# Pairs of key heads and partition groups of samples in a hybrid decoder layer

## Chip, cores and metric

The kernel runs on one core of a Trainium2 chip. The metric is device microseconds of one execution. TensorE is called PE in the rows, its weight loads PEld, VectorE DVE, ScalarE ACT, GpSimd POOL, and the queue that issues most transfers SP.

## What is computed

One layer of a decoder: 512 prompt tokens and 8 samples of one token each (with 2048 past positions) go through the same weights. Four mixers (two gated linear attentions A and B, pooling C, sparse attention D) are gated, projected and added, then an MLP follows. The change touches the sample's step of A and B, and D:

```python
# A, B, per sample: S = S * exp(log_f) + k v^T ; o = S^T q
o = jnp.einsum('bthk,bhkv->bthv', qd, S)
# D: 8 query heads in 2 groups (key heads) of 4, head dimension 64; three branches, each a softmax over its keys
sc = jnp.einsum('bqhgd,bchd->bqhgc', qb, kc)      # compressed keys, one per 16 tokens
ss = jnp.einsum('bqhgd,bhqkpd->bqhgkp', qb, ks)   # selected blocks of 64 tokens, top 16 (prompt: all are selected)
sw = jnp.einsum('bqhgd,bkhd->bqhgk', qb, wb[:, :, 0])   # window of 512
o  = gb[..., 0:1] * o_cmp + gb[..., 1:2] * o_slc + gb[..., 2:3] * o_win
```

All data are fp32. For the 512 prompt tokens the selected and the window branch are both causal attention with keys and values of their own.

## The kernel before

Each engine has its own program, and they meet at semaphores. TensorE's program alternates between two kinds of work. The first is the **special work** of the mixers, written out in order. The second is **dense work**: projections with 128x1024 weight tiles, each product made of three matmuls in a reduced fp32 format (high x high, low x high, high x low; a "triple", L618 to L624; L651 for outputs by token). `tick(name, i)` stands in every engine's program at the same places: on TensorE it makes triples until a table (`CUM`, from the quotas of `SECTIONS`, L169) is met, on SP it loads weight tiles whose slot came free (`LD_AT`), one tick later ScalarE casts them to the high part (`upper`, L1179, the cast is L1183), one more tick later GpSimd makes the low part (`lower`, L2126). VectorE or ScalarE evacuate the dense units that end in that tick (`EVAC_AT`): branch units by VectorE (L1475 with L1478), gates by ScalarE. When the last branch unit of a mixer ends (`B_END`), ScalarE casts the next mixer's output (`branch_upper`) and VectorE subtracts (`branch_lower`, L1490). A dense unit starts when the unit two before it is evacuated.

**Samples of A and B** (L786 to L798): for each of four head pairs `k`, eight samples `x` accumulate a 16x128 product in PSUM partitions 0 to 15; VectorE copies it (`OSS`, L1663), four transposes follow.

**Compressed scores of D** (L875 to L885): for each key head `k`, which lies on 64 of the 128 rows of the array, and each 128 tokens `i`, four matmuls; VectorE adds the mask.

**Attention** (L907 to L940, 64 `UNITS` of one head, one branch and 128 tokens `i`): in iteration `u` TensorE makes the scores of unit u (K = 64, 128 to 512 columns), the transposes of u-2, the products with the values of u-3, and tick u. VectorE (L1827 on) adds the causal mask and takes the maximum of u, and copies the transposed u-2; ScalarE (L1359 on) makes the exponential of u. The scores of u wait until the exponential of u-2 is done. After 16 units VectorE normalises and adds the outputs of these 128 tokens (L1846 to L1862), for which the values' products of the next 128 tokens wait. GpSimd meanwhile gathers and sums cached rows for the samples.

**Samples of D** (`s6`): round 0 is the window branch, round 1 the selected one. The scores of the eight samples are made and copied; `softmax_of_round` on VectorE and ScalarE (with `sums_of_round` on TensorE) takes maximum, exponential and sum; then each sample x accumulates its 8x128 (L1043 to L1050) or 8x64 (L1078 to L1087) product in PSUM partitions 0 to 7, one sample after the other, with a tick after every four or every one; VectorE copies it into `SO` (L2013, L2045), eight transposes follow, and the result is added to `OACC`. In round 0 VectorE's tick 25 stands after `softmax_of_round`, in round 1 its tick 39. When all sums of round 1 are done, SP reloads x and goes on with the weights. After `s6` come the last projections and the MLP, which the change leaves alone.

## Time and profile before

| | |
|---|---|
| median of three runs | 1400.93 us (1395.85 to 1408.07) |
| profiled execution | 1402.41 us, its span 1400.5 us |
| busy share | PE 92%, PEld 86%, DVE 45%, POOL 41%, ACT 25% |
| granted TensorE clock | mean 0.957 of full speed |
| attention (`att`) | from 496.6 to 714 us of the span |
| samples of D (`s6`) | from 718 to 966.6 us |

Times in the rows are microseconds from the start of the span. A timeline row merges instructions of one kind that follow each other: its second number reaches from the first start to the last end, and ends overlap the next instruction's start. An fp32 matmul appears as two instructions. The granted clock has two levels, 1.2 and 2.4 GHz; a number between 0.5 and 1 is a mix over a stretch.

### The profile page before, as it was taken

The numbers are of one execution on the slowest core, as the hardware profiler recorded it, in microseconds if no ns is written. First come the engines' busy times: TensorE is split into PE (matmuls) and PEld (weight loads), VectorE is DVE, ScalarE is ACT, GpSimd is POOL, SyncE is SP. The second block draws the span as 40 slices with busy tenths as digits, with TensorE's granted clock in tenths as the row PEclk, the third lists the DMA queues.
The fourth block names the chain that finished last, engine by engine and source line by source line (L and its number), as shares of the span: only waits on it lengthen the run. The fifth ranks groups of instructions, "written<-read, shape, count | busy, mean of one in ns | idle before, by whom it ended". The sixth has DMA issues, their size and how long they took to land.

```text
span 1400.5 us, 23708 instructions
## 1 busy us (share of the span) xinstructions
PE 1294.8 (92%) x10276; PEld 1205.1 (86%) x10276; DVE 635.9 (45%) x1026; ACT 350.2 (25%) x518; POOL 578.0 (41%) x433
## 2 busy tenths in 40 slices
PE   4989999997858899999997999897999999999999
PEld 4989999886758787877787988886999999999999
DVE  6245655525364444455554532314738710177400
ACT  4231222200451233332322121211332211222210
POOL 1443653311163167656512334221536544455542
PEclk9999999997998898999998999988999999999999
DMA  4311121040322143332341325213222323223232
GB/s 181 105 61 61 60 62 56 36 98 31 105 61 93 38 153 127 137 120 76 106 161 50 113 69 196 61 46 122 91 91 91 91 91 91 91 91 93 95 97 95
DMA packets 42909, 129.31 MB, mean 92 GB/s; under 512 B 3958, under 2 KB 15006, under 8 KB 40621
## 3 DMA queue, kind: packets, MB, share of 16 engines
q1 hardware_dynamic: 38197, 102.62, 23.0%
q0 software_dynamic: 4608, 25.17, 5.0%
q8 instruction: 82, 1.34, 0.4%
q14 instruction: 22, 0.18, 0.0%
HBM read 121.64 MB, written 6.36 MB: 91 GB/s over the span
## 4 chain that ended last, share of the span: by engine, by line
PE 84%; DVE 8%; DMA 4%; ACT 2%; issue 1%; SPq 1%; DVEq 0%; ACTq 0%
PE PS L622 19%; PE PS L624 18%; PE PS L623 18%; PE PS L651 9%; PE PS L914 3%; PE PS L937 2%; DMA M<-w_tiles 2%; PE PS L727 2%; PE PS L923 2%; PE PS L1082 1%; PE PS L1070 1%; DMA M<-state_hgrn 1%; PE PS L763 1%; PE PS L765 1%; PE PS L882 1%
## 5 line engine op out<-in xcount | busy, mean ns | idle before, releaser
L2132 POOL TENSOR_TENSOR WL<-M,WH 128x512 fp32r<-128x512 f32 x314 | 426.4, 1382 | 720.2 <-ACT WH L1183 719.8
L622 PE MATMUL PS<-hH,WH 128*128 128x260 f32 x1360 | 406.6, 299 | 23.5 <-DVE M L1470 13.5
L624 PE MATMUL PS<-hH,WL 128*128 128x260 f32 x1360 | 393.0, 289 | 1.5 <-issue 1.5
L623 PE MATMUL PS<-hL,WH 128*128 128x260 f32 x1360 | 393.0, 289 | 0.0
L622 PEld LDWEIGHTS PS<-hH,WH 128*128 128x128 f32 x1360 | 266.5, 196 | 29.8 <-issue 26.2
L624 PEld LDWEIGHTS PS<-hH,WL 128*128 128x128 f32 x1360 | 265.7, 195 | 1.2 <-issue 1.2
L1183 ACT CAST WH<-M 128x1024 fp32r<-128x1024 f32 x159 | 165.9, 1046 | 402.7 <-DMA M<-w_tiles 267.7
L623 PEld LDWEIGHTS PS<-hL,WH 128*128 128x128 f32 x1360 | 266.0, 196 | 0.5
L624 PE MATMUL PS<-uH,WL 128*128 128x260 f32 x512 | 144.7, 283 | 0.0
L622 PE MATMUL PS<-uH,WH 128*128 128x260 f32 x512 | 144.6, 282 | 0.0
L623 PE MATMUL PS<-uL,WH 128*128 128x260 f32 x512 | 144.1, 281 | 0.0
L651 PE MATMUL PS<-WH,hH 128*128 128x256 f32 (+1 forms) x360 | 107.3, 298 | 10.9 <-DVE M L1461 10.9
L651 PE MATMUL PS<-WH,hL 128*128 128x256 f32 (+1 forms) x360 | 103.2, 287 | 0.0
L651 PE MATMUL PS<-WL,hH 128*128 128x256 f32 (+1 forms) x360 | 103.0, 286 | 0.0
L622 PEld LDWEIGHTS PS<-uH,WH 128*128 128x128 f32 x512 | 96.4, 188 | 0.0
L624 PEld LDWEIGHTS PS<-uH,WL 128*128 128x128 f32 x512 | 96.3, 188 | 0.0
L623 PEld LDWEIGHTS PS<-uL,WH 128*128 128x128 f32 x512 | 96.3, 188 | 0.0
L622 PE MATMUL PS<-BH,WH 128*128 128x260 f32 x256 | 77.9, 304 | 8.5 <-DVE OL L2062 8.2
L2118 DVE TENSOR_TENSOR M<-M,PS 128x520 f32<-128x520 f32 x16 | 11.1, 696 | 163.5 <-PE PS L624 163.5
L651 PEld LDWEIGHTS PS<-WH,hH 128*128 128x128 f32 (+1 forms) x360 | 62.8, 174 | 21.1 <-issue 16.5
L624 PE MATMUL PS<-BH,WL 128*128 128x260 f32 x256 | 73.9, 289 | 0.0
L1365 ACT ACTIVATE M<-PS,stat 128x128 f32<-128x128 f32 (+3 forms) x64 | 33.8, 527 | 133.9 <-DVE stat L1836 133.7
(368 smaller groups left out, 2088.9 us busy)
## 6 DMA issues: line engine op xcount, KB each, us to landing
M<-w_tiles SPq DMA_DIRECT2D x159, 512.0 KB, 3.6
M<-x_T SPq DMA_DIRECT2D x8, 520.0 KB, 5.5
M<-cache_win_kv SPq DMA_DIRECT2D x2, 2048.0 KB, 11.2
y_T<-M SPq DMA_DIRECT2D x8, 260.0 KB
con<-tables SPq DMA_DIRECT2D x1, 1475.5 KB, 12.1
M<-state_gla SPq DMA_DIRECT2D x2, 512.0 KB, 8.7
M<-state_hgrn SPq DMA_DIRECT2D x2, 512.0 KB, 11.7
gla_sample<-M SPq DMA_DIRECT2D x2, 512.0 KB, 6.8
```

The costliest lines, as they stand in the source:

```text
L622: mm(out, hi[:, cols], x_hi, start=first, stop=False)
L623: mm(out, hi[:, cols], x_lo, start=False, stop=False)
L624: return mm(out, lo[:, cols], x_hi, start=False, stop=last_k)
L651: last = mm(PS[0:m, BANK[u], 0:256], x[:, k, t], w, start=(k == 0 and x is hH and w is hi), stop=(k == KT - 1 and x is hL))
L727: last = mm(PS[:, row(q + par), 128 * k:128 * k + 128], a, a, start=True, stop=True)
L763: last = mm(o, zv[:, c, head_cols(k, par)[0]], SC[:, 2 * c + par, k], start=True, stop=(c == 0))
L914: mm(PS[:, bank, 0:128 * i + 128], QT[r, g, 128 * i:128 * i + 128], (KTS, KTW)[b][r, 0:128 * i + 128], start=True, stop=True).then_inc(sem ...
L923: last = tr(PS[:, 4 + v % 2, 128 * j:128 * j + 128], P[v % 3][:, 128 * j:128 * j + 128], ident)
L937: last = mm(PS[:, 6 + b, out], PT[v % 3][:, j], zn[:, j, col:col + out.stop - out.start], start=(j == 0), stop=(j == i))
L1183: nc.scalar.copy(WH8[s], WR[s]).then_inc(sem("w_hi"), 1)
L1365: f(P[u % 3][:, 0:128 * i + 128], PS[:, 2 + u % 2, 0:128 * i + 128], ACT.Exp, bias=nm[u % 3], accum_out=rs[:, i, b, h:h + 1]).then_inc(sem ...
L2132: last = p.tensor_tensor(WL8[s][:, c], WR[s][:, c], WH8[s][:, c], ALU.subtract)
```

## The change

In the four places the order of matmuls is changed so that neighbouring ones use different parts of the array. The units of attention are reordered so that two neighbours belong to different key heads; TensorE issues both scores of a pair, then a tick, transposes of u-2, values of u-3, transposes of u-1, a tick, values of u-2; VectorE takes both maxima of a pair, then the tick, then the copies. Attention gets one more tick (68). The compressed scores alternate between the key heads. The sample sums put their products in four groups of 32 PSUM partitions, neighbours in different groups; VectorE clears `OSS` and `SO` and copies four pieces, and one transpose of 128 partitions (two in D) takes the place of four (eight). VectorE's ticks 25 and 39 move ahead of the rounds' softmax. The ranges of ticks of the other engines follow.

```diff
-            ("att", 67, 4), ("s6", 50, 7))
+            ("att", 68, 4), ("s6", 50, 7))
...
+        OSS = EL[0][:, 1536:1664]
...
+        SO = M[:, 35168:35424]
...
+        cs_bank = lambda i, k: ((4, 5), (2, 3))[i % 2][k]
...
-        UNITS = [(i, b, h) for i in range(TT) for b in range(2) for h in (7, 6, 5, 4, 0, 1, 2, 3)]
+        UNITS = [(i, b, h) for i in range(TT) for b in range(2) for h in (7, 0, 6, 1, 5, 2, 4, 3)]
...
-            for k in range(4):
-                for x in range(NS):
-                    last = mm(PS[0:16, 2, 128 * k:128 * k + 128], QM[:, 128 * k + 16 * x:128 * k + 16 * x + 16],
+            for x in range(NS):
+                for k in range(4):
+                    last = mm(PS[32 * k:32 * k + 16, 2, 0:128], QM[:, 128 * k + 16 * x:128 * k + 16 * x + 16],
                               SS[:, k // 2, x, k % 2], start=(x == 0), stop=(x == NS - 1))
             last.then_inc(once("os_mm"), 1)
             tick("smp", 8)
             pe.wait_ge(*done("oss"))
-            for k in range(4):
-                last = tr(PS[:, 3, 16 * k:16 * k + 16], OSS[:, 128 * k:128 * k + 128], ident[0:16, 0:16])
-            last.then_inc(once("ost_mm"), 1)
+            tr(PS[:, 3, 0:128], OSS, ident).then_inc(once("ost_mm"), 1)
             tick("smp", 9)
...
+            for i in range(TT):
+                if i >= 2:
+                    pe.wait_ge(sem("cs_ev"), 2 * i - 2)
+                for g in range(G):
+                    for k in range(HKV):
+                        r = slice(64 * k, 64 * k + 64)
+                        last = mm(PS[:, cs_bank(i, k), 32 * g:32 * g + 32], QT[r, g, 128 * i:128 * i + 128],
                                   kcT[r, :], start=True, stop=True)
-                    last.then_inc(sem("cs_mm"), 1)
-                tick("cmp", 3 + k)
+                last.then_inc(sem("cs_mm"), 2)
+                if i % 2:
+                    tick("cmp", 3 + i // 2)
...
-            for u in range(NU + 3):
+            def scores_of_pair(u):
+
+                if u >= 2:
+                    pe.wait_ge(sem("ex"), u)
+                for w in (u, u + 1):
+                    i, b, h = UNITS[w]
+                    k, g = h // G, h % G
+                    r = slice(64 * k, 64 * k + 64)
+                    mm(PS[:, 2 + w % 2, 0:128 * i + 128], QT[r, g, 128 * i:128 * i + 128],
+                       (KTS, KTW)[b][r, 0:128 * i + 128], start=True, stop=True).then_inc(sem("s_mm"), 1)
+
+            def transposes_of(v):
+
+                i = UNITS[v][0]
+                pe.wait_ge(sem("ex"), v + 1)
+                if v >= 2:
+                    pe.wait_ge(sem("pt_ev"), v - 1)
+                for j in range(i + 1):
+                    last = tr(PS[:, 4 + v % 2, 128 * j:128 * j + 128], P[v % 3][:, 128 * j:128 * j + 128], ident)
+                last.then_inc(sem("t_mm"), 1)
...
+            def values_of(v):
+
+                i, b, h = UNITS[v]
+                pe.wait_ge(sem("pt_ev"), v + 1)
+                if v % 16 == 0 and i:
+                    pe.wait_ge(sem("on"), i)
+                col = (CS, CW)[b] + 128
+                out = slice(64 * h - 64 * (h // G), 64 * h - 64 * (h // G) + (64 if h == 3 else 128))
...
+            for u in range(0, NU + 4, 2):
                 if u < NU:
-                    i, b, h = UNITS[u]
-                    k, g = h // G, h % G
-                    r, bank = slice(64 * k, 64 * k + 64), 2 + u % 2
-                    if u >= 2:
-                        pe.wait_ge(sem("ex"), u - 1)
-                    mm(PS[:, bank, 0:128 * i + 128], QT[r, g, 128 * i:128 * i + 128],
-                       (KTS, KTW)[b][r, 0:128 * i + 128], start=True, stop=True).then_inc(sem("s_mm"), 1)
+                    scores_of_pair(u)
+                tick("att", u)
                 if 2 <= u < NU + 2:
-                    v = u - 2
-                    i = UNITS[v][0]
-                    pe.wait_ge(sem("ex"), v + 1)
-                    if v >= 2:
...
+                    transposes_of(u - 2)
+                if 4 <= u < NU + 4:
+                    values_of(u - 3)
+                if 2 <= u < NU + 2:
+                    transposes_of(u - 1)
+                tick("att", u + 1)
+                if 2 <= u < NU + 2:
+                    values_of(u - 2)
...
-                for j in range(NS):
-                    last = tr(PS[:, 6, 128 + 8 * j:136 + 8 * j], SO[:, 128 * j:128 * j + 128], ident[0:8, 0:8])
+                for j in range(2):
+                    last = tr(PS[:, 6, 128 + 128 * j:256 + 128 * j], SO[:, 128 * j:128 * j + 128], ident)
...
-            for x in range(NS):
-                o = PS[0:8, o_bank(x), 128 * (x % 4):128 * (x % 4) + 128]
+            for n in range(2):
+                o = [PS[32 * j:32 * j + 8, 7, 128 * n:128 * n + 128] for j in range(4)]
                 for i in range(4):
-                    mm(o, SXB[1][:, x, i], wtile(x, i)[1], start=(i == 0), stop=False)
-                mm(o, SN[1][:, 8 * x:8 * x + 8], zn[0:NS, 4, CW + 128:CW + 256], start=False, stop=True)\
-                    .then_inc(sem("sv_mm"), 1)
-                if x % 4 == 3:
-                    tick("s6", 27 + x // 4)
+                    for j in range(4):
+                        mm(o[j], SXB[1][:, 4 * n + j, i], wtile(4 * n + j, i)[1], start=(i == 0), stop=False)
+                for j in range(4):
+                    x = 4 * n + j
+                    last = mm(o[j], SN[1][:, 8 * x:8 * x + 8], zn[0:NS, 4, CW + 128:CW + 256],
+                              start=False, stop=True)
+                last.then_inc(sem("sv_mm"), 4)
+                tick("s6", 27 + n)
...
-            for x in range(NS):
-                pe.wait_ge(sem(f"xv{x}"), 16)
-                o = PS[0:8, 7, 64 * x:64 * x + 64]
+            for n in range(2):
+                o = [PS[32 * j:32 * j + 8, 7, 64 * n:64 * n + 64] for j in range(4)]
+                for j in range(4):
+                    pe.wait_ge(sem(f"xv{4 * n + j}"), 16)
                 for i in range(16):
-                    mm(o, SX[:, x, i], XV[x][:, 64 * i:64 * i + 64], start=(i == 0), stop=False)
+                    for j in range(4):
+                        x = 4 * n + j
+                        mm(o[j], SX[:, x, i], XV[x][:, 64 * i:64 * i + 64], start=(i == 0), stop=False)
+                    if i % 4 == 3 and i < 15:
+                        tick("s6", 41 + 4 * n + i // 4)
                 for k in range(HKV):
                     col = CS + 128 + 64 * k
-                    last = mm(o, SNK[k][:, 8 * x:8 * x + 8], zn[0:NS, 4, col:col + 64], start=False, stop=(k == 1))
-                last.then_inc(sem("sv_mm"), 1)
-                tick("s6", 41 + x)
+                    for j in range(4):
+                        x = 4 * n + j
+                        last = mm(o[j], SNK[k][:, 8 * x:8 * x + 8], zn[0:NS, 4, col:col + 64],
+                                  start=False, stop=(k == 1))
+                last.then_inc(sem("sv_mm"), 4)
+                tick("s6", 44 + 4 * n)
...
+            step(v.memset(OSS, 0.0))
...
-            v.tensor_copy(OSS, PS[0:16, 2]).then_inc(once("oss"), 1)
+            for k in range(4):
+                r = slice(32 * k, 32 * k + 16)
+                ins = v.tensor_copy(OSS[r], PS[r, 2, 0:128])
+                if k < 3:
+                    step(ins)
+                else:
+                    ins.then_inc(once("oss"), 1)
...
+            for i in range(TT):
+                dve.wait_ge(sem("cs_mm"), 2 * i + 2)
+                neg = C("cmpneg", 32 * i, 32 * i + 32).unsqueeze(1).to_broadcast([128, 4, 32])
+                for k in range(HKV):
                     v.tensor_tensor(CM[:, i, 4 * k:4 * k + 4],
-                                    PS[:, (4, 5, 2, 3)[i], 0:128].rearrange("p (h c) -> p h c", h=4),
+                                    PS[:, cs_bank(i, k), 0:128].rearrange("p (h c) -> p h c", h=4),
                                     neg, ALU.add).then_inc(sem("cs_ev"), 1)
-                tick("cmp", 3 + k)
+                if i % 2:
+                    tick("cmp", 3 + i // 2)
...
+            def maximum_of(u):
+
+                i = UNITS[u][0]
+                dve.wait_ge(sem("s_mm"), u + 1)
+                if u >= 3:
+                    dve.wait_ge(sem("ex"), u - 2)
...
+                    .then_inc(sem("mx"), 1)
+
+            for u in range(NU + 4):
+                if u % 2 == 0 and u < NU:
+                    maximum_of(u)
+                    maximum_of(u + 1)
+                if u % 2 == 0:
+                    tick("att", u)
                 if 2 <= u < NU + 2:
...
-                tick("att", u)
+                if u % 2:
+                    tick("att", u)
...
+                o = PS[:, 6, 128:384].rearrange("p (x c) -> p x c", c=32)[:, :, 0:8]
+                step(v.tensor_tensor(OT.rearrange("p (x h) -> p x h", h=8), o,
+                                     COEF.rearrange("p (x h) -> p x h", h=8), ALU.mult))
...
+            tick("s6", 25)
             softmax_of_round(0, 1)
-            tick("s6", 25)
             tick("s6", 26)
             dve.wait_ge(sem("sv_mm"), NS)
-            for j in range(2):
-                ins = v.tensor_copy(SO[:, 512 * j:512 * j + 512], PS[0:8, o_bank(4 * j)])
-                if j == 0:
+            step(v.memset(SO, 0.0))
+            for j in range(4):
+                r = slice(32 * j, 32 * j + 8)
+                ins = v.tensor_copy(SO[r], PS[r, 7, 0:256])
+                if j < 3:
                     step(ins)
                 else:
                     ins.then_inc(sem("so"), 1)
...
+            tick("s6", 39)
             softmax_of_round(1, 0)
-            tick("s6", 39)
...
+            for j in range(4):
+                r = slice(32 * j, 32 * j + 8)
+                ins = v.tensor_copy(SO[r].rearrange("p (n a d) -> p n a d", n=2, a=2),
+                                    PS[r, 7, 0:128].rearrange("p (n d) -> p n d", n=2).unsqueeze(2)
+                                    .to_broadcast([8, 2, 2, HD]))
+                if j < 3:
+                    step(ins)
+                else:
+                    ins.then_inc(sem("so"), 1)
```

## Rows read from the trace of the kernel before

**Rows 1.** The page's part 4, shares of the chain that ended last.
```profile
PE 84%; DVE 8%; DMA 4%; ACT 2%; issue 1%; SPq 1%; DVEq 0%; ACTq 0%
```

**Rows 2.** Timeline of PE in attention: start us, us to last end, what.
```profile
507.40 0.49 PE L914 MATMUL PS<-M 64*128 64x128 f32 x2
507.82 0.33 PE L923 MATMUL PS<-con,M 128*128 128x128 f32 x1
...
509.75 0.48 PE L914 MATMUL PS<-M 64*128 64x128 f32 x2
...
663.42 1.12 PE L914 MATMUL PS<-M 64*128 64x512 f32 x2
664.47 0.66 PE L923 MATMUL PS<-con,M 128*128 128x128 f32 x4
...
667.38 1.12 PE L914 MATMUL PS<-M 64*128 64x512 f32 x2
```

**Rows 3.** Timeline of PE, four runs of small matmuls, two halves by turns or one.
```profile
128.89 1.16 PE L727 MATMUL PS<-M 64*128 64x128 f32 x16
...
246.42 1.09 PE L749 MATMUL PS<-M 128*64 128x128 f32 x16
...
343.99 7.16 PE L790 MATMUL PS<-M 128*16 128x128 f32 x64
...
463.45 3.75 PE L882 MATMUL PS<-stat,M 64*128 64x32 f32 x32
...
468.77 4.22 PE L882 MATMUL PS<-stat,M 64*128 64x32 f32 x32
```

**Rows 4.** Page part 6, timelines of SP and ACT, lines by form, in attention.
```profile
M<-w_tiles SPq DMA_DIRECT2D x159, 512.0 KB, 3.6
...
508.77 0.80 SPq L516 DMA_DIRECT2D M<-w_tiles  x2
...
513.73 1.05 ACT L1183 CAST WH<-M 128x1024 fp32r<-128x1024 f32 x1 [0.20 <-DMA M<-w_tiles]
...
590.96 0.33 SPq L516 DMA_DIRECT2D M<-w_tiles  x1
...
599.40 1.05 ACT L1183 CAST WH<-M 128x1024 fp32r<-128x1024 f32 x1 [4.92 <-DMA M<-w_tiles]
...
L1835 DVE TENSOR_TENSOR PS<-PS,con 128x128 f32<-128x128 f32 x64 | 19.1, 299 | 98.3 <-PE PS L914 98.1
...
L1365 ACT ACTIVATE M<-PS,stat 128x128 f32<-128x128 f32 x16 | 5.9, 367 | 25.3 <-DVE stat L1836 25.2
```

**Rows 5.** Waits of PE in attention: us in total, times, longest.
```profile
PE PS L937 <- DVE M L1858: 6.1, 3, 3.3
```

**Rows 6.** Timeline of PE in both rounds of sums of the samples.
```profile
837.57 1.04 PE L1046 MATMUL PS<-M 128*8 128x128 f32 x8
838.54 0.38 PE L1047 MATMUL PS<-M,gaT 8*8 8x128 f32 x2
838.85 0.39 PE L622 MATMUL PS<-hH,WH 128*128 128x260 f32 x1
...
952.83 1.95 PE L1082 MATMUL PS<-M 128*8 128x64 f32 x32
...
955.03 0.38 PE L622 MATMUL PS<-BH,WH 128*128 128x260 f32 x1
```

**Rows 7.** Timeline of DVE around round 0's maximum.
```profile
820.57 0.62 DVE L1969 TENSOR_REDUCE gaT<-M 128x64 f32<-128x256 f32 x1
...
831.54 0.43 DVE L1478 TENSOR_TENSOR M<-M,tmp 128x260 f32<-128x260 f32 x1
831.89 2.49 DVE L1490 TENSOR_TENSOR OL<-M,BH 128x512 fp32r<-128x512 f32 x4
```

**Rows 8.** Timeline of PE after round 1's sums, idle time and releaser in brackets.
```profile
966.64 0.56 PE L622 MATMUL PS<-BH,WH 128*128 128x260 f32 x1 [8.24 <-DVE OL L2062]
```

**Rows 9.** Windows: engines busy us (instructions), granted clock, DMA share, GB/s.
```profile
538.00:556.00 18.00, 14.68 (x74) 12.18 (x74) 9.70 (x22) 6.29 (x15) 9.82 (x8) 0.72 0.41 167
```

More of the change, by code:

```diff
@@ L397, in build @@
         QM = EL[0][:, 1024:1536]
-        OSS = EL[0][0:16, 1536:2048]
+        OSS = EL[0][:, 1536:1664]
         KQS = M[:, SP0:SP0 + 64].rearrange("p (k s) -> p k s", k=8)
@@ L587, in _ @@
                 tick("cmp", i)
-            for i in range(67):
+            for i in range(68):
                 tick("att", i)
@@ L906, in _ @@
             pe.wait_ge(*done("gd"))
-            for u in range(NU + 3):
-                if u < NU:
-                    i, b, h = UNITS[u]
-                    k, g = h // G, h % G
-                    r, bank = slice(64 * k, 64 * k + 64), 2 + u % 2
-                    if u >= 2:
-                        pe.wait_ge(sem("ex"), u - 1)
-                    mm(PS[:, bank, 0:128 * i + 128], QT[r, g, 128 * i:128 * i + 128],
-                       (KTS, KTW)[b][r, 0:128 * i + 128], start=True, stop=True).then_inc(sem("s_mm"), 1)
-                if 2 <= u < NU + 2:
-                    v = u - 2
-                    i = UNITS[v][0]
-                    pe.wait_ge(sem("ex"), v + 1)
-                    if v >= 2:
-                        pe.wait_ge(sem("pt_ev"), v - 1)
-                    for j in range(i + 1):
-                        last = tr(PS[:, 4 + v % 2, 128 * j:128 * j + 128], P[v % 3][:, 128 * j:128 * j + 128], ident)
-                    last.then_inc(sem("t_mm"), 1)
-                if u >= 3:
-                    v = u - 3
-                    i, b, h = UNITS[v]
-                    pe.wait_ge(sem("pt_ev"), v + 1)
-                    if v % 16 == 0 and i:
-                        pe.wait_ge(sem("on"), i)
-                    col = (CS, CW)[b] + 128
-                    out = slice(64 * h - 64 * (h // G), 64 * h - 64 * (h // G) + (64 if h == 3 else 128))
-                    for j in range(i + 1):
-                        last = mm(PS[:, 6 + b, out], PT[v % 3][:, j], zn[:, j, col:col + out.stop - out.start],
-                                  start=(j == 0), stop=(j == i))
-                    last.then_inc(sem("pv_mm"), 1)
-                tick("att", u)
@@ new lines, in values_of @@
+            def values_of(v):
[5 more added lines that the diff above has]
+                out = slice(64 * h - 64 * (h // G), 64 * h - 64 * (h // G) + (64 if h == 3 else 128))
+                for j in range(i + 1):
+                    last = mm(PS[:, 6 + b, out], PT[v % 3][:, j], zn[:, j, col:col + out.stop - out.start],
+                              start=(j == 0), stop=(j == i))
+                last.then_inc(sem("pv_mm"), 1)
@@ L1358, in _ @@
                 tick("cmp", i)
-            for u in range(NU + 3):
+            for u in range(NU + 4):
                 if u < NU:
@@ L1824, in _ @@
                     ins.then_inc(once("gd"), 1)
-            for u in range(NU + 3):
-                if u < NU:
-                    i = UNITS[u][0]
-                    dve.wait_ge(sem("s_mm"), u + 1)
-                    if u >= 3:
-                        dve.wait_ge(sem("ex"), u - 2)
-                    diagonal = PS[:, 2 + u % 2, 128 * i:128 * i + 128]
-                    step(v.tensor_tensor(diagonal, diagonal, C("causal"), ALU.add))
-                    v.tensor_reduce(nm[u % 3], PS[:, 2 + u % 2, 0:128 * i + 128], AX, ALU.max, negate=True)\
-                        .then_inc(sem("mx"), 1)
+            def maximum_of(u):
[3 more added lines that the diff above has]
+                    dve.wait_ge(sem("ex"), u - 2)
+                diagonal = PS[:, 2 + u % 2, 128 * i:128 * i + 128]
+                step(v.tensor_tensor(diagonal, diagonal, C("causal"), ALU.add))
+                v.tensor_reduce(nm[u % 3], PS[:, 2 + u % 2, 0:128 * i + 128], AX, ALU.max, negate=True)\
+                    .then_inc(sem("mx"), 1)
+            for u in range(NU + 4):
+                if u % 2 == 0 and u < NU:
[3 more added lines that the diff above has]
+                    tick("att", u)
                 if 2 <= u < NU + 2:
@@ L1862, in _ @@
                             ins.then_inc(sem("on"), 1)
-                tick("att", u)
+                if u % 2:
+                    tick("att", u)
             dve.wait_ge(sem("c_red"), 8)
@@ L2216, in _ @@
             gp.wait_ge(sem("qt_mm"), 5)
-            for u in range(NU + 3):
+            for u in range(NU + 4):
                 x = u // 8
```

21 lines of the change are left out of this document (2 added, 19 removed).

## The prediction, on record before the change was run

> **What bounds the kernel.** I read the chain of waits first: 84% of it is TensorE [rows 1], so a microsecond taken from TensorE's own row counts, unless a wait takes its place. Then the timeline of TensorE in the four places that the change touches. In attention a unit costs TensorE 2.35 us in the first 128 tokens (507.40 to 509.75) and 3.96 us in the last (663.42 to 667.38), always in the same rhythm: scores, transposes, values, 12 dense matmuls; the scores hold it 0.42 us there and 1.05 us here before the first transpose starts [rows 2]. By straight line between these ends the four blocks of tokens have 0.42, 0.63, 0.84, 1.05 us of scores and units of 2.35, 2.89, 3.43, 3.96 us. In the whole stage TensorE waits for VectorE only 6.1 us, three times, at the block ends [rows 5].
>
> **Do groups overlap?** The same rows answer it. A score matmul of K=64 on one half of the rows costs 3.75/32 = 117 ns an instruction where all 32 use one half (L882), and 1.16/16 = 73 ns where the halves take turns (L727). Outputs: 7.16/64 = 112 ns where all go to the first 16 partitions (L790), 1.09/16 = 68 ns where they alternate between partitions 0 and 64 (L749) [rows 3]. Less some 0.2 us of start and drain for a run, that is two at the price of one. Four groups at once no row shows: the bounds are four in the time of one, and two. I take four, as weights of 8 or 16 columns occupy little of the array and the two-group rows overlap fully.
>
> **Term by term.**
> - Samples' state sums (L790): 64 instructions of 7.16 us become 16 rounds of 0.11 us and a start, 1.96 us: **-5.2** (two groups: -3.4). One transpose for four: -0.1. VectorE copies four pieces, each in a dependent step of some 0.3 us as L1835 takes [rows 4], for one copy; TensorE's dense tick 8 (15 matmuls of some 0.12 us) lies beside them, so nothing; uncovered it would be under 1 us. The memset of OSS is done while the states are still loading: nothing.
> - Compressed scores (L882): 3.75 and 4.22 us [rows 3] become twice 16 rounds at L727's price, 1.16 + 8 x 0.11 = 2.05 us: -3.9. VectorE ends with two additions in place of one, +0.3: **-3.6** (bounds -3.6 and 0).
> - Attention: 32 pairs, each saves the scores of one unit: 8 x (0.42 + 0.63 + 0.84 + 1.05) = **-23.5** (bounds: that and 0). The dense work now also stands between scores and transposes; the number of changes of shape in a pair does not rise, so nothing. Iteration 68 only brings four triples of dense work forward.
> - Attention, new waits. A pair's scores now wait for the exponential of both units before (`ex` >= u, where it was u - 1), so ScalarE's queue counts. At even ticks it casts freshly loaded weights between the two exponentials of a pair. After the first double load is issued (T = 508.77) the second cast ends at 514.78, T + 6.0 [rows 4]; exponential u+1 (0.37 us [rows 4]) stands behind it, so the next scores start at T + 6.4. TensorE is there at T + 4.5: a pair is 2 x 2.35 - 0.42 = 4.3 us, and one unit's values. Wait: 2.0 us. The single load in that block casts at 3.6 us to landing [rows 4] + 1.05: 0.6 us. One double load in the second block, where a pair is 5.15 us: 1.0. In the later blocks a pair of 6.0 to 6.9 us covers the chain. One load lands late, I think because GpSimd's gather moves rows then: issued 590.96, cast ends 600.45, T + 9.5 [rows 4]; with the exponential T + 10.1, against T + 6.6 for TensorE: 3.5 us, of which the wait at that block end is there already (half of the 6.1 - 3.3 us of the two short ones, 1.4 [rows 5]): +2.1. The double load at the first block end meets a gather too, I price it likewise, one cast longer: +2.1 over the 3.3 us that this end costs now [rows 5]. Sum **+7.8** (bounds: 0, if the loads land earlier, and 14).
> - Window sums, round 0 (L1046): 1.28 us for each of eight samples [rows 6] become 2 x 1.28: -7.7; eight small transposes become two, -0.3: **-8.0** (two groups: -5). SO's memset and four copies take some 2.3 us on VectorE; tick 28, 21 dense matmuls of 0.12 us or more, covers them.
> - The moved tick 25. With four triples more before it, its quota now reaches the end of both branch units, so VectorE must do two evacuations of two operations and the four subtractions of L1490 before the maximum, where now it takes the maximum (820.57) under running dense work and the evacuations (to 834.38) under the next dense work [rows 7]. No DMA or other queue moves with it. After the last branch triple: evacuation 0.9 us (two operations like the 0.43 of L1478), four subtractions 2.49, maximum 0.62: TensorE, which has one triple of its own (0.36) left, waits **+3.6** (bounds 2.5, the evacuation lying under the own triple and the subtractions, and 4.5). The moved tick 39 holds nothing for VectorE: only gates end there, and ScalarE takes those.
> - Selected sums, round 1 (L1082, L1085): 2.20 us a sample [rows 6], 17.6 for eight and 0.5 more in the first one at half clock, become 2 x 2.20 and some restarts after dense ticks, 0.6: **-13.1** (bounds -13.1, and -1 below). The last branch weights get less lead, but 16 triples and values still give about 7 us, and of these a landing of 3.6 and a cast of 1.05 [rows 4] leave 2.4 for GpSimd's lowering: nothing (at worst 1). The last four copies lie beside the reload that TensorE waits 8.2 us for after these sums [rows 8]; that load starts when the sums end, so the gain passes through.
> - Clock. After the 3.3 us wait at the first block end the stretch 538 to 556 ran at a granted 0.72, a mix of the 1.2 and 2.4 GHz levels [rows 9]. It lost 18 x 0.28 = 5 us of clock, 4.1 of it in busy time (14.68 of 18). I charge one such stretch to the wait grown to 3.5 us, and half of one (2) to round 0: **+6** (bounds 0, if it does not fall, and 12).
>
> Sum: -5.3 - 3.6 - 23.5 + 7.8 - 8.0 + 3.6 - 13.1 + 6 = **-36**. The profiled execution took 1402.4 us (span 1400.5), 1.5 above the median of the runs: **1366 us**.
>
> A rule on the selected sums. Their rows are 1.95/32 = 61 ns an instruction alone [rows 6], and the two-group runs start their pairs far closer than one matmul lasts [rows 3]. The Trainium skill, TensorEngine Tiling (Array Packing), "Instruction Overhead", says each matmul has about 60 cycles of overhead and that a tiling factor should not be taken from a dimension already small. By it I estimate 25 ns a start at 2.4 GHz, so four 64-column passes take 100 ns and not 61, and round 1 gives some 3 us less: 1369. No run here shows four groups, so the trace neither agrees nor differs yet.
>
> **Rivals.**
> 1. *All waits stay covered.* Loads land sooner as TensorE asks in another rhythm, and the clock holds: only the 3.6 us of tick 25 remains, -50: 1353. For it: the chain of a pair without casts is short, two additions, two maxima and two exponentials of about 0.3 to 0.4 us each [rows 4], well inside 4.3 us. Against: the casts' landing times. 15%.
> 2. *The start rate binds the partition groups.* No row shows instructions starting at less than 55 to 68 ns on average [rows 3, 6]. At 55 ns round 1 keeps 288 x 0.055 = 16 us, a gain of 2 for 13.1; round 0's 80 give -5, the state sums -3.4: 1366 + 16 = 1382, and between that and 1366 for a lower floor. Against: light weights, 64 columns. 15%, the rule's middle case with it.
> 3. *Attention gives its gain back.* The pair is only as early as its later exponential, ScalarE's casts come late more often than the rows of four loads tell, and low clock follows. Break-even of the stage is a mean wait of 23.5/32 = 0.73 us a pair; I have 0.25. At 0.73: 1366 + 15 = 1381; with two more low stretches 1390. 12%.
> 4. *Slower: changing the group drains the array.* Each change of shape costs about 0.1 us (L1047's two passes of 0.11 need 0.31 of the 1.28 [rows 6]). If a hop to another partition group paid that and nothing overlapped, the 32 + 32 + 40 + 144 matmuls of the four sums and scores would pay 25 us, and the new waits and clock 18: 1402 + 43 = 1445. It decides as soon as overlap is worth less than the 18. Against: L727 and L749 hop at every matmul and overlap [rows 3]. 4%.
> 5. *The pairs overlap only in part*, one pass of the two, since passes of 512 columns are issued one unit after the other: half of 23.5 is lost, 1378. L727 hops at the same grain with 128 columns. 4%.
>
> My forecast keeps 50%.
>
> **Numbers.** Likeliest 1366. Eight in ten: from 1350 (rival 1 and a little more clock) to 1388 (rivals 2, 3 and 5). A measurement of this kernel tells about 1%, 14 us, from no change. Faster by more than that (under 1387): the forecast, rivals 1, 2 and 5 and a part of 3, less for what I have not seen: 0.84. Within: 0.11. Slower: rival 4 and a tail of 3: 0.05.
>
> **What would show it.** Right: L790's line lasts about 2 us, L882's two lines 2 each, pairs of scores in the last block under 1.2 us for both units, L1046's 64 in two runs of about 1 us, L1082's 256 in some 4 us; a wait of about 3.6 us ahead of round 0's sums for L1490; some five waits of TensorE in attention that end with an exponential behind a cast. Wrong: four-group lines that last half of the old time or more (rivals 2, 4), a wait before most pairs (3), no wait ahead of round 0's sums.

## The result and the profile after

The changed kernel takes 1348.72 us (median of four runs, 1343.22 to 1351.48) against 1401.98 for the kernel before on the same chip: ratio 0.9615, 95% interval [0.9562, 0.9669]. Five more runs of it (below) gave 1349.08 and 0.9634 [0.9613, 0.9655]. I forecast 1366, 36 us less than before; it is 53 less, just outside my range of 1350 to 1388. The profiled execution took 1350.24 us, its span is 1348.4.

The chain of waits of the changed kernel, shares of the span (answers to [rows 1]):

```profile
PE 82%; DVE 8%; DMA 5%; ACT 2%; issue 2%; SPq 1%; POOL 0%; DVEq 0%; ACTq 0%
```

TensorE is still what bounds the kernel. Its timeline at the four places, answering to [rows 3, 6, 8] (start, us to the last end, what):

```profile
343.20 1.94 PE L790 MATMUL PS<-M 128*16 128x128 f32 x64
...
458.27 1.98 PE L879 MATMUL PS<-stat,M 64*128 64x32 f32 x32
...
461.81 1.98 PE L879 MATMUL PS<-stat,M 64*128 64x32 f32 x32
...
472.56 0.69 PE L889 MATMUL PS<-con,M 128*128 128x128 f32 x2 [7.14 <-DVE M L1826]
...
805.19 1.06 PE L1058 MATMUL PS<-M 128*8 128x128 f32 x32
806.18 0.40 PE L1061 MATMUL PS<-M,gaT 8*8 8x128 f32 x8
...
882.88 0.63 PE L1099 MATMUL PS<-M 128*8 128x64 f32 x32
...
914.91 0.56 PE L622 MATMUL PS<-BH,WH 128*128 128x260 f32 x1 [9.41 <-DVE OL L2110]
```

Four groups cost the time of one: 64 state sums last 1.9 us instead of 7.2, four samples of round 0 one sample's 1.06, and 32 instructions of round 1 last 0.63 us instead of 1.95. Behind the compressed scores TensorE now waits 7.14 us, where it waited 3.8 before; that I had not forecast. The kernel before, its waits there and at the end of attention (us in all, times, longest):

```profile
PE PS L891 <- DVE M L1795: 3.8, 1, 3.8
PE PS L945 <- DVE M L1858: 3.3, 1, 3.3
```

Attention, answering to [rows 2]:

```profile
506.02 0.49 PE L913 MATMUL PS<-M 64*128 64x128 f32 x4 [1.24 <-ACT M L1387]
506.44 0.39 PE L622 MATMUL PS<-hH,WH 128*128 128x260 f32 x1
...
510.17 0.49 PE L913 MATMUL PS<-M 64*128 64x128 f32 x4
...
640.62 1.13 PE L913 MATMUL PS<-M 64*128 64x512 f32 x4
641.68 0.39 PE L622 MATMUL PS<-hH,WH 128*128 128x260 f32 x1
...
647.42 1.13 PE L913 MATMUL PS<-M 64*128 64x512 f32 x4
```

Both units' scores hold TensorE 0.42 us in the first block and 1.06 in the last, what one unit's did. A pair takes 4.15 and 6.80 us (I had 4.3 and 6.9). TensorE's waits in the stage, answering to [rows 5] (us in all, times, longest):

```profile
PE PS L935 <- DVE M L1895: 9.1, 3, 3.2
PE PS L913 <- DVE gaT L1851: 2.4, 1, 2.4
PE PS L913 <- ACT M L1387: 2.2, 2, 1.2
PE PS L956 <- DVE M L1895: 1.5, 1, 1.5
```

The block ends now cost 9.1 us (6.1 before), the exponentials behind casts 2.2, and the end of the stage 1.5 (3.3 before). VectorE ahead of round 0's sums, answering to [rows 7]:

```profile
787.49 0.43 DVE L1500 TENSOR_TENSOR M<-M,tmp 128x260 f32<-128x260 f32 x1
787.84 2.49 DVE L1512 TENSOR_TENSOR OL<-M,BH 128x512 fp32r<-128x512 f32 x4
790.25 0.59 DVE L2007 TENSOR_REDUCE gaT<-M 128x64 f32<-128x256 f32 x1
```

The maximum stands behind the four subtractions, and TensorE waits 3.55 us for it, as priced.

**Where the 52 us of the span are.** I counted, stretch by stretch, TensorE's idle time and its busy time at the lower clock level in both traces. Idle time rose from 102.4 to 114.6 us (+12.2). Busy time at 1.2 GHz fell from 85.6 to 69.1; half of it is lost, so -8.3. The rest, the work itself, is -56.0. My forecast had +11.7 of waits, +6 of clock and -53.8 of work. A second trace of each kernel (e10 and e1, below), counted likewise, has +11.0 of waits, 0 of clock (70.4 and 70.2 us) and -56.3 of work: waits and work repeat, the clock does not.

### The profile page after: what moved, and what is told of

Same layout as the page of the kernel before. It is cut to its first block, busy times and chain, and to the rows that moved or that the text cites. A ratio compares the mean times of both kernels' runs of the same rounds, so it can differ in the third digit from the quotient of the medians.

```text
span 1348.4 us, 23691 instructions
## 1 busy us (share of the span) xinstructions
PE 1230.6 (91%) x10261; PEld 1164.0 (86%) x10261; DVE 641.6 (48%) x1036; ACT 349.7 (26%) x518; POOL 579.3 (43%) x433
## 3 DMA queue, kind: packets, MB, share of 16 engines
q1 hardware_dynamic: 38197, 102.62, 23.5%
## 4 chain that ended last, share of the span: by engine, by line
PE 82%; DVE 8%; DMA 5%; ACT 2%; issue 2%; SPq 1%; POOL 0%; DVEq 0%; ACTq 0%
PE PS L622 20%; PE PS L624 19%; PE PS L623 18%; PE PS L651 9%; DMA M<-w_tiles 4%; PE PS L935 2%; PE PS L727 2%; PE PS L913 2%; PE PS L1084 1%; PE PS L923 1%; DMA M<-state_hgrn 1%; PE PS L763 1%; PE PS L765 1%; PE PS L1076 1%; PE PS L782 1%
## 5 line engine op out<-in xcount | busy, mean ns | idle before, releaser
L622 PEld LDWEIGHTS PS<-hH,WH 128*128 128x128 f32 x1360 | 262.3, 193 | 39.5 <-issue 35.5
L623 PEld LDWEIGHTS PS<-hL,WH 128*128 128x128 f32 x1360 | 262.3, 193 | 0.4
L624 PEld LDWEIGHTS PS<-hH,WL 128*128 128x128 f32 x1360 | 262.1, 193 | 0.4 <-issue 0.4
L651 PEld LDWEIGHTS PS<-WL,hH 128*128 128x128 f32 (+1 forms) x360 | 63.6, 177 | 1.9
```

The source lines that it names most:

```text
L622: mm(out, hi[:, cols], x_hi, start=first, stop=False)
L623: mm(out, hi[:, cols], x_lo, start=False, stop=False)
L624: return mm(out, lo[:, cols], x_hi, start=False, stop=last_k)
L651: last = mm(PS[0:m, BANK[u], 0:256], x[:, k, t], w, start=(k == 0 and x is hH and w is hi), stop=(k == KT - 1 and x is hL))
```

## Experiments

### The same two kernels again

The changed kernel (e1) and the kernel before (e10), unaltered.

> The changed kernel once more, unaltered, for a narrow ratio and a second trace. Theory (the waits and the clock that I charged did not come, because the order of the work sets them): ratio 0.960 to 0.964, and a second trace shows the low stretches of the granted clock at the same places, 95 to 108 us in all as in the first (101.6). Rival (the low stretches fall by chance from one execution to the next): places differ, and the total may be anything between 90 and 125 us.

> The kernel before once more, unaltered, for a second trace of its granted clock. Theory (the low stretches follow waits that recur at the same places, with lengths that differ by a few us): about 120 us of low clock again, of which 14 to 20 us between attention and round 0, against 7 to 14 in the changed kernel, and 13 us behind the compressed scores, against 7. Rival (the first trace was a bad draw): 100 to 106 us, as in the changed kernel, and the clock is no part of the gain.

Measured: e1 1349.08 us, ratio 0.9634; e10 1394.56 us, one run. Windows of attention and of the stretch from there to round 0's sums in four traces: before, before again, after, after again (PE busy, PEld, DVE, ACT, POOL, granted clock, DMA share, GB/s):

```profile
496.56:718.38 221.82, 212.46 (x1412) 174.33 (x1412) 114.12 (x262) 69.82 (x175) 130.10 (x104) 0.97 0.33 117
718.38:825.25 106.87, 96.63 (x727) 94.87 (x727) 47.80 (x96) 21.27 (x32) 32.54 (x27) 0.91 0.32 109
```

```profile
493.58:714.71 221.13, 212.61 (x1413) 174.29 (x1413) 113.98 (x262) 69.74 (x175) 129.94 (x104) 0.97 0.33 117
714.71:818.03 103.32, 92.77 (x726) 90.80 (x727) 47.21 (x96) 21.16 (x32) 33.09 (x27) 0.93 0.33 113
```

```profile
488.98:686.51 197.53, 184.61 (x1424) 165.09 (x1424) 115.77 (x262) 70.27 (x176) 131.16 (x104) 0.98 0.37 131
686.51:790.90 104.39, 90.46 (x727) 88.30 (x727) 52.51 (x104) 22.88 (x35) 32.14 (x27) 0.97 0.34 121
533.00:551.00 18.00, 16.42 (x118) 14.88 (x119) 10.48 (x25) 5.75 (x17) 16.99 (x15) 0.91 0.24 90
577.00:595.00 18.00, 15.10 (x104) 12.41 (x103) 9.58 (x20) 3.64 (x10) 12.65 (x11) 0.91 0.37 136
```

```profile
485.22:684.71 199.49, 187.49 (x1424) 167.27 (x1424) 115.67 (x262) 69.92 (x176) 131.09 (x105) 0.97 0.36 130
684.71:790.40 105.69, 92.89 (x726) 90.52 (x726) 51.49 (x104) 22.87 (x35) 31.64 (x26) 0.94 0.34 119
```

The same stretch of the same kernel ran at 0.91 and at 0.93, or at 0.97 and at 0.94. The low time of a whole record, some 2 us behind the span's end counted in, was 121.8 and 104.9 us before, 101.6 and 107.6 after. Most low stretches recur at the same places, but how many there are and how long differs, and e10's rival holds in its first half: the trace that I priced the clock from was a bad draw. Its granted clock is 0.957; the 29 runs of the kernel before here lie between 0.955 and 0.965, mean 0.9596. The nine of the changed kernel have 0.962. Span times lost clock makes 56.5 us before and 51.0 after. The change costs no clock; on average it gives back some 5 us, part of them idle time, so the rival's other half, that the clock is no part of the gain, does not hold over all runs.

The block ends show my error at its place. The stretch behind the first, from which I had the price, ran at 0.72 before, behind a wait of 3.3 us [rows 9], with a low stretch of 10.2 us in this trace and again in e10; after, behind waits of 3.24 and 2.74 us, it ran at 0.91, with 3.4 us of low clock in both traces. The second block end, to which I had charged such a stretch, waits 2.90 us after, and 3.4 us of low clock follow in both traces (577 to 595 above, 0.91); before, behind 1.16 us, there were none. Waits of much the same length, unequal stretches; what decides the length stays open.

### The order undone: one group at a time

```diff
-            for x in range(NS):
-                for k in range(4):
+            for k in range(4):
+                for x in range(NS):
...
-        UNITS = [(i, b, h) for i in range(TT) for b in range(2) for h in (7, 0, 6, 1, 5, 2, 4, 3)]
+        UNITS = [(i, b, h) for i in range(TT) for b in range(2) for h in (7, 6, 5, 4, 0, 1, 2, 3)]
```

and the same exchange of loops in the compressed scores and both rounds.

> The changed kernel with the order inside each run of small matmuls undone: same products, same partitions, same ticks and copies, but all of one group before the next, and units of attention paired within one key head, so that neighbours use the same part of the array. Theory (the gain is overlap and nothing else): +5.2 state sums, +4.0 compressed scores of which about 3 are hidden by a wait for VectorE that is there anyway, +23.5 attention, +6 round 0, +12.7 round 1, less 1 to 3 for waits now covered: 1393 to 1400 us, ratio 0.994 to 0.999 of the kernel before. Rival (the new order in attention, ticks between scores and transposes and fewer copies, saves by itself): a third of the gain stays, 1380 or less, ratio 0.985.

Measured: 1383.48 us, ratio 0.9888 [0.9852, 0.9924]. Neither theory: the order is worth 34 us, and 19 of the 53 stay without it. Its timeline (attention's pair, state sums, rounds 0 and 1):

```profile
340.22 5.90 PE L790 MATMUL PS<-M 128*16 128x128 f32 x64
...
665.05 1.98 PE L913 MATMUL PS<-M 64*128 64x512 f32 x4
...
821.29 2.38 PE L1058 MATMUL PS<-M 128*8 128x128 f32 x32
...
906.12 1.95 PE L1099 MATMUL PS<-M 128*8 128x64 f32 x32
```

Three things keep the 19 us. First, two units side by side in one key head take 1.91 us to the next instruction, not 2 x 1.05: summed over the stage at the full clock, scores cost 47.0 us before, 40.7 here and 23.7 in the changed kernel, so of the 23.3 saved 6.2 come from putting two units together and 17.1 from overlap. Second, a run ends fewer times: attention has 259 runs of one kind of work before and 226 after, one change less for each pair, and the transposes, values and dense runs got some 3 us shorter together (four triples that the added tick brings forward left out); round 0's and round 1's last small products (0.31 us for each sample) became 0.33 for four. Third, some overlap is left: the 64 state sums last 5.9 us and not 7.16, and 32 instructions of round 0 take 2.31 us to the next instruction and not 4 x 0.97, since at each change of group the new group starts before the old one is done (next experiment). With longer pairs the block ends also wait less, 5.8 us.

### How far TensorE reaches past a waiting instruction

```diff
-            for x in range(NS):
-                for k in range(4):
+            for x, k in [(x + d, k) for x in range(0, NS, 2) for k in range(4) for d in range(2)]:
+                if True:
```

This is e5's state sums; rounds 0 and 1 have orders of the same kind, told in the expectation.

> The changed kernel with another order inside the sums: state sums with two matmuls of a partition group in a row before the next group; round 0 with two groups taking turns and then the other two; round 1 with two matmuls of a group in a row for the first four samples and four in a row for the last four. Theory (read from start times: TensorE starts an instruction out of the next four that wait if its group is free; one group's instructions follow each other at 109 ns for 128 columns and 56 for 64, different groups at 7): worked through, and with the 0.10 us that ends each run, the state sums last 2.28 us (1.87 when all take turns, 5.83 one at a time), a run of round 0 1.57 (0.99 and 2.31), a run of round 1 0.76 in the first four samples and 1.24 in the last four (0.56 and 1.88). Rival (overlap is a matter of which groups are in the run, not of their order): 1.87, 0.99, 0.56. Rival (neighbours alone can overlap): state sums about 3.9, round 1 1.0 and 1.4. Total about 1349 + 0.4 + 1.2 + 0.8 + 2.7 = 1354 us.

Measured (state sums, round 0, round 1's first and last four samples):

```profile
339.84 1.97 PE L790 MATMUL PS<-M 128*16 128x128 f32 x64
...
804.47 1.50 PE L1058 MATMUL PS<-M 128*8 128x128 f32 x32
...
883.33 0.65 PE L1098 MATMUL PS<-M 128*8 128x64 f32 x32
...
894.22 1.31 PE L1098 MATMUL PS<-M 128*8 128x64 f32 x32
```

To the next instruction these are 1.90, 1.43, 0.58 and 1.24 us. My theory has only the last right; two matmuls in a row cost almost nothing, four in a row do. A theory that gives all of these, and the 5.83 and 2.31 of e2: instructions are handed out in order, and each partition group takes up to four, the running one counted. An fp32 matmul is two instructions, so two in a row fit. It was put to a new order, e12:

```diff
-            for x in range(NS):
-                for k in range(4):
+            for x, k in [(x, k) for b in ((0, 1, 2), (3, 4, 5), (6, 7)) for k in range(4) for x in b]:
+                if True:
...
```

> The changed kernel with a third order inside the sums: state sums with three, three and then two matmuls of a partition group in a row; round 1 with two groups taking turns for four matmuls each and then the other two. Theory after the runs of two (each partition group takes up to four instructions, the running one counted, instructions are handed out in order, and a matmul is two instructions): worked through with 109 and 56 ns an instruction and 0.10 us for the end of a run, the state sums last 2.77 us and a run of round 1 0.80. Rival (my first theory, four waiting instructions over all groups): 3.12 and 0.90. Rival (a few matmuls more or less in a row do not matter): 1.90 and 0.58. Total about 1349 + 0.9 + 1.9 = 1352 us.

Measured, state sums and one run of round 1:

```profile
341.22 2.91 PE L790 MATMUL PS<-M 128*16 128x128 f32 x64
...
882.98 0.86 PE L1098 MATMUL PS<-M 128*8 128x64 f32 x32
```

That is 2.84 and 0.79 us to the next instruction, against 2.77 and 0.80 expected and 3.12 and 0.90 of the rival. Four to a group it is, within 3%: by the same reckoning I estimate 3.5 us for these state sums with three to a group, and 2.2 with five. It fits halves of the rows too: in e2 the first 32 compressed scores, with eight instructions of one half in a row, take 2.43 us to the next instruction where taking turns takes 1.91, and the reckoning, at their 112 ns an instruction, gives 2.37.

### Each half of the change alone

e3 is the kernel before with the samples' sums and the compressed scores changed, e4 the one with attention, its tick and the moved ticks 25 and 39.

> The kernel before with the state sums, the compressed scores and both rounds' sums changed, and attention, the number of its ticks and VectorE's ticks 25 and 39 as before. Theory: -5.2 state sums, -1 to -2.4 compressed scores (the rest goes into a longer wait for VectorE behind them), -6 to -8 round 0, -12.7 to -14 round 1: 1372 to 1377 us, ratio 0.979 to 0.983. Rival (the clock's 20 us less of low stretches come from these places, not from attention): 5 us more, 1367 to 1371, ratio 0.976 to 0.978.

> The kernel before with attention in pairs, its 68 ticks and VectorE's ticks 25 and 39 moved, and the four sums and scores of the samples and compressed keys as before. By the prices on record (-23.5 overlap, +7.8 waits, +3.6 the moved tick 25, +4 to 6 clock): -6 to -8, 1394 to 1396 us, ratio 0.995. Theory now (waits +3.4, clock no worse or better): -20 to -25, 1377 to 1382 us, ratio 0.982 to 0.986, with a wait of about 3.5 us ahead of round 0's sums.

Measured: e3 1369.15 us, ratio 0.9775 [0.9738, 0.9812]; e4 1377.71 us, 0.9821 [0.979, 0.9853]. Against 1402.29 these are -33 and -25; they add up to -58 where both together give -53, within the intervals. e3 lies where its rival has it (1367 to 1371), but its interval does not tell that from its theory; e4 is in its theory's range (1377 to 1382). My prices on record make -30 for the first (near) and -6 to -8 for the second. e4's trace, counted as above against the one of before, has +7.1 us of waits (priced 11.4), 0 of clock (priced 4 to 6) and -26 of work (priced -23.5). So attention's side of the sum, with the clock that I had charged there, is where the forecast failed.

### The waits, one at a time

**e6**, the first product with a new block's values a pair later:

```diff
+                if u % 16 == 4 and 4 < u < NU + 4:
+                    values_of(u - 4)
...
-                if 2 <= u < NU + 2:
+                if 2 <= u < NU + 2 and (u % 16 != 2 or u == 2):
                     values_of(u - 2)
```

> The changed kernel, but TensorE makes the first product with the values of a new block of 128 tokens (the one that waits for VectorE's normalisation of the block before) one pair of units later. Theory (the three waits of 3.2, 2.9 and 3.0 us at the block ends are VectorE's three microseconds of normalisation, and the work of a pair covers them): the three waits go, at most 1 us in all stays as a wait of the scores; 1340 to 1343 us against 1349. Rival (the wait moves: VectorE is then behind with maxima and copies, and the scores or transposes of the next pairs wait the same time): 1347 to 1350.

Measured: 1339.45 us, ratio 0.9578 [0.9529, 0.9627]. Its waits in attention:

```profile
PE PS L913 <- ACT M L1389: 5.6, 4, 2.3
PE PS L913 <- DVE gaT L1853: 2.5, 1, 2.5
PE PS L958 <- DVE M L1897: 1.5, 1, 1.5
PE PS L935 <- DVE M L1883: 0.8, 1, 0.8
```

Both theory and rival hold in part: the 9.1 us are 0.8, and 3.4 come back as scores that wait for an exponential. Attention takes 192.0 us (197.5 and 199.5), at a granted clock of 0.99.

**e7**, tick 25 back:

```diff
-    for _ in range(_n):
-        CUM.append((CUM[-1] if CUM else 0) + _quota)
+    for _i in range(_n):
+        CUM.append((CUM[-1] if CUM else 0) + (0 if (_name, _i) == ("att", 56) else _quota))
...
-            tick("s6", 25)
             softmax_of_round(0, 1)
+            tick("s6", 25)
```

> The changed kernel with one of attention's 68 ticks (the 56th) left empty, so that the last branch unit ends in tick 26 of the samples' section as in the kernel before, and VectorE's tick 25 again behind round 0's maximum. Dense work is moved, none left out. Theory: the wait of 3.55 us ahead of round 0's sums goes, and the low stretch of the granted clock of 10.2 us that follows it shrinks to about 3.4 us as in the kernel before: -4 to -6, 1343 to 1345 us. Rival (the maximum then stands behind other work and the wait comes back as another): no change, 1348 to 1350. Rival (the clock does not depend on that wait): -3.5, 1345 to 1346.

Measured: 1345.08 us, ratio 0.9614 [0.9574, 0.9654]. The wait ahead of round 0's sums is gone, the low stretch behind it is 3.4 us instead of 10.2, and the stretch from there to the transposes takes 16.4 us instead of 18.2. In the medians it is the expected 4 us; the ratio alone does not tell it from e1.

**e8**, dense work ahead of the compressed scores' softmax, and **e9**, GpSimd held back there:

```diff
-    for _ in range(_n):
-        CUM.append((CUM[-1] if CUM else 0) + _quota)
+    for _i in range(_n):
+        CUM.append((CUM[-1] if CUM else 0) + (_quota if (_name, _i) < ("cmp", 4) or _name != "cmp" else 12 if _i == 4 else 3 if _i < 7 else 2))
```

```diff
             for i in range(10):
+                if i == 5:
+                    gp.wait_ge(*done("cp"))
                 tick("cmp", i)
```

> The changed kernel with eight triples of dense work moved ahead of the compressed scores' softmax (tick 4 of that section has 12 triples, ticks 5 to 9 have 3, 3, 2, 2, 2, where all had 4). Theory (what the faster compressed scores save runs into VectorE's chain of reduce, subtract, exponential, sum and product, 8 us after the last score, so TensorE waits 7.1 us): the wait falls by the 8 x 0.36 = 2.9 us, of which the thinner ticks behind give back up to 1: 1346 to 1347 us; VectorE's two operations on 128x1024 still last 2.2 us each beside GpSimd. Rival (the chain's end moves with the work put before it): no change, 1348 to 1350.

> The changed kernel with GpSimd's low parts of two weight tiles held back until VectorE's softmax of the compressed scores is done. Theory (VectorE's subtraction and product on 128x1024 last 2.24 and 2.17 us in the changed kernel, against 1.40 and 1.23 before, because GpSimd works on two operands from the same memory at that time; in the kernel before they fell between): both last about 1.23, TensorE's wait ahead of the transposes falls from 7.1 to about 5.2 us; total 1347 to 1348. Rival (the operations are slower for another reason, as their data come from freshly written places): both stay at 2.2, the wait at 7.1.

Measured: e8 1342.81 us, ratio 0.9609 [0.9569, 0.9648], its wait 4.4 us and its stretch (from the first score to attention) 27.4 us instead of 30.7; the other 3 us of its median may go with the clock (mean 0.9645 in its runs, 0.9614 in e1's), and the ratio alone does not tell it from e1. e9 1347.52 us, one run. VectorE's softmax and GpSimd beside it, before, after and in e9:

```profile
474.61 1.40 DVE L1792 TENSOR_TENSOR M<-M,stat 128x1024 f32<-128x1024 f32 x1
...
478.39 1.23 DVE L1795 TENSOR_TENSOR M<-M,con 128x1024 f32<-128x1024 f32 x1
...
472.42 5.95 POOL L2132 TENSOR_TENSOR WL<-M,WH 128x512 fp32r<-128x512 f32 x4 [20.42 <-ACT WH L1183]
```

```profile
465.61 2.24 DVE L1823 TENSOR_TENSOR M<-M,stat 128x1024 f32<-128x1024 f32 x1
...
470.33 2.17 DVE L1826 TENSOR_TENSOR M<-M,con 128x1024 f32<-128x1024 f32 x1
...
465.50 5.92 POOL L2180 TENSOR_TENSOR WL<-M,WH 128x512 fp32r<-128x512 f32 x4 [18.37 <-ACT WH L1205]
```

```profile
463.98 1.22 DVE L1823 TENSOR_TENSOR M<-M,stat 128x1024 f32<-128x1024 f32 x1
467.47 1.22 DVE L1825 TENSOR_REDUCE stat<-M 128x32 f32<-128x1024 f32 x1 [2.26 <-ACT M L1378]
468.73 1.23 DVE L1826 TENSOR_TENSOR M<-M,con 128x1024 f32<-128x1024 f32 x1
...
470.03 4.96 POOL L2180 TENSOR_TENSOR WL<-M,WH 128x512 fp32r<-128x512 f32 x4 [24.88 <-DVE M L1826]
```

With GpSimd out of the way both operations last 1.2 us: after the faster scores VectorE's chain meets more of GpSimd's four low parts, which costs it 1.8 us. Before, the two operations did not fall clear of them, as my expectation of e9 says: GpSimd worked beside the chain there too, but one of its operations ended 0.32 us after the subtraction began, and all four before the product; in e10 the subtraction lasted 1.92 us, which leaves 1.3 of the 1.8. In e9 the wait falls to 6.2 us and not to 5.2, because the exponential between them is then late by another us (2.26 against 1.23): ScalarE casts two tiles until 465.1 and then loads a table for 1.28 us (ACT_TABLE_LOAD). The one time of e9 is no more than the noise away from e1's. The Trainium skill, SBUF — State Buffer, section "SBUF: two separate sides", says that a VectorE operation with two inputs in SBUF and a GpSimd operation that reads SBUF hold one port pair by turns, each for its whole length; the traces agree, 2.24 us being nearly 1.22 and the 1.16 left of a GpSimd operation of 1.27 that had begun 0.11 us earlier.

**e11**, all four:

> The changed kernel with all four edits: the first product with the values of a block one pair later, tick 25 back behind the maximum with one empty tick in attention, eight triples moved ahead of the compressed scores' softmax, and GpSimd's low parts held back there. By the runs of each alone (-9.6, -4, -4 to -6, -1 to -2 us): 1328 to 1332 us, ratio 0.948 to 0.952 of the kernel before, and faster than the changed kernel by 1.2 to 1.6%. Rival (they cover the same time twice, as the dense work moved forward is missed elsewhere): 1336 to 1339, no better than the first of them alone.

Measured: 1335.61 us (six runs, 1328.16 to 1341.37), ratio 0.9533 [0.9491, 0.9575]. Two of its waits:

```profile
PE PS L964 <- DVE M L1903: 3.3, 1, 3.3
PE PS L628 <- POOL WL L2188: 2.8, 2, 1.6
```

It beats both kernels, but the changed one by 13 us and not the 17 to 21 expected: TensorE now waits 2.8 us for low parts of weights that GpSimd makes later, and the end of attention costs 3.3 us again. Idle time is 102.5 us, that of the kernel before. The time lies between theory and rival, and the intervals do not tell it from e6, the first of the four edits alone.

## Why the prediction was wrong, step by step

- **Do groups overlap: right.** Four at the price of one. State sums -5.3 as forecast; at the full clock, round 0 -8.1 (forecast -8.0); round 1's sums -12.4 (forecast -13.1); the attention scores -23.3 (forecast -23.5), though only 17.1 of these are overlap.
- **"The number of changes of shape in a pair does not rise, so nothing": wrong by some 3 us.** It falls by one for each pair.
- **Compressed scores, "bounds -3.6 and 0": the rows are 4.0 us shorter, the wait behind them 3.4 longer.** I had followed VectorE only to its last addition, not through the softmax, where GpSimd works: from the last score to the transposes it is now 8.8 us (6.8 before, 7.3 in e10), and the four triples between, at the low clock before, cover 1.7 us instead of 3.0.
- **Attention, new waits, +7.8: +3.5 in the trace.** The first double load's cast cost 1.24 us (priced 2.0), a late load in the last block 1.0; these two, and not some five, end with an exponential behind a cast. The first block end did not grow (3.24, priced 5.4); the second and third did, by 1.7 (priced 2.1) and 1.4 (priced 0), but these waits end with VectorE's normalisation (L1895, and e6), not with the cast that I had priced. The wait at the end of the stage fell by 1.8, which I had not counted: the added tick lies under the last normalisation.
- **The moved tick 25, +3.6: right**, 3.55 us, at its place and with its releaser.
- **Nothing for the selected sums' last loads: right** within 0.4 us (one dense run in round 1 took 3.07 us, the others 2.70 to 2.76). The reload behind them waits 9.4 us instead of 8.2.
- **"Clock. I charge one such stretch to the wait grown to 3.5 us, and half of one (2) to round 0. +6": this is the step that failed.** In the two profiles the clock gave 8.3 us back, 14.3 of the 16 us by which the profiled sum missed; in the second traces it gave 0, and over all runs it gave some 5. In none of these did it cost the 6 us that I charged. I priced a stretch from one trace as if a wait of that length always brought it. Where I charged it, the second block end, 3.4 us of low clock came and not 10.2, a loss of 1.6 us of work for my 4; round 0's half came as told (10.2 us of low clock for 3.4, a loss of 2.3 for my 2). And I had only added low stretches (0 was my lower bound), while others go: the first block end lost 2.6 us less than before, and between attention and round 0, where the change leaves TensorE's matmuls alone, busy time at 1.2 GHz was 17.7 and 8.8 us in the two traces before, 3.3 and 8.1 in the two after. The profiled execution of before, at 0.957 where the mean is 0.9596, also made the base of the sum some 3 us too slow.

The waits in sum, +11.7 forecast and +12.2 counted, were right by luck: attention's were half of what I said, and the compressed scores' wait made up for it.

Rival 1 has the nearest time (1353) for a wrong reason: the waits grew. Rival 2 is out: starts of different groups come 7 ns apart. So are 3 (a mean wait of 0.4 us a pair in all), 4 and 5.

## What to carry over

Small matmuls that use different partition groups or halves of rows cost here what one group costs, if no more than two fp32 matmuls of a group follow each other. After such a gain follow the next engine's chain to its end: what it runs beside has moved too. Price the clock from several executions, and let it come out either way.

## What the runs showed of the hardware

In the changed kernel's state sums four instructions start 7 ns apart, and the next four follow every 109 ns (the second four after 120); in round 1 it is 7 and 56 ns. 64 columns take 56 ns and 128 take 109, so no fixed part of an instruction shows in a run, and 32 instructions of round 1 come every 17.6 ns on average (0.564 us). The Trainium skill, TensorEngine Tiling (Array Packing), section "Instruction Overhead", gives about 60 cycles of overhead for each matmul, from which I had estimated 25 ns a start at 2.4 GHz; the trace differs, and the measurement decides. Each group holds up to four instructions (e5, e12), so the order inside a run need not alternate strictly.
